# Two key pages per vector instruction in a decoder step

## The reference

```
h += W_o( sig(g_a) * U_a(stick-breaking attention) + sig(g_b) * U_b(GLA) )
h += PEER(rmsnorm(h))            # product-key experts: top 16 of 16384 for each of 8 heads
h += (p W_ple) * sigmoid(rmsnorm(h) W_ple_gate)
```

```
z[h, s]    = q[h] . k[s, h] / sqrt(64) + bias[h]
A[h, s]    = sigmoid(z[h, s]) * prod over later j of (1 - sigmoid(z[h, j]))
out[h]     = sum over s of A[h, s] * v[s, h]
```

## Time and profile before

| | us |
|---|---|
| median of 3 runs | 2529.41 (2528.65 to 2534.58) |
| the profiled execution | 2528.97 |
| its span, first to last instruction | 2527.3 |
| PE busy | 2043.2 |
| DVE busy | 1417.8 |
| POOL busy | 977.5 |
| ACT busy | 641.2 |

### The profile page before, as it was taken

One profiled execution on the slowest core, in us unless ns is written; L12 is line 12 of the kernel. 1 busy time (PEld: TensorE's weight loads), 2 busy tenths in 40 slices (PEclk: granted clock), 3 DMA queues, 4 the chain that ended last, 5 costly groups with the idle time before them and its releaser, 6 DMA issues.

```text
span 2527.3 us, 25588 instructions
## 1 busy us (share of the span) xinstructions
PE 2043.2 (81%) x6090; PEld 1018.0 (40%) x6090; DVE 1417.8 (56%) x2800; ACT 641.2 (25%) x1753; POOL 977.5 (39%) x1422
## 2 busy tenths in 40 slices
PE   7999965787778999947777777887778877688778
PEld 6746850143334738823232322333233333233322
DVE  3698898513211215976665556555566555666442
ACT  2202220201443012112233232232322332323321
POOL 0233333002222000025666555654555644566540
PEclk9999988977888999979999999999999999999999
DMA  3568779763443323149999999999999999999991
GB/s 120 182 206 287 253 259 350 252 194 118 140 153 132 103 68 113 50 167 413 408 418 421 422 388 413 386 385 420 421 387 411 368 422 422 385 404 400 372 422 58
DMA packets 139984, 738.89 MB, mean 292 GB/s; under 512 B 19112, under 2 KB 19544, under 8 KB 72312
## 3 DMA queue, kind: packets, MB, share of 16 engines
q0 software_dynamic: 105632, 645.98, 64.5%
q1 hardware_dynamic: 34272, 91.91, 10.9%
HBM read 732.26 MB, written 5.56 MB: 292 GB/s over the span
## 4 chain that ended last, share of the span: by engine, by line
PE 35%; DMA 25%; issue 13%; DVE 10%; POOL 6%; ACT 5%; POOLq 4%; SPq 1%; ACTq 0%; DVEq 0%
DMA arena<-experts_in,arena 22%; PE bank L1533 11%; DVE arena L121 6%; PE bank L1477 4%; POOLq L482 4%; POOL arena L507 4%; PE bank L1502 3%; PE bank L1440 3%; DVE arena L1148 3%; PE bank L1427 2%; ACT arena L121 2%; PE bank L1198 2%; POOL arena L503 1%; PE bank L1287 1%; DMA arena<-cache_v_in 1%
## 5 line engine op out<-in xcount | busy, mean ns | idle before, releaser
L1533 PE MATMUL bank<-arena 128*128 128x512 f32 x2048 | 980.7, 628 | 303.2 <-ACT arena L768 303.0
L1148 DVE CUSTOM_DVE_ANT_0 arena<-arena 128x1024 f32<-128x1024 f32 x512 | 626.5, 1230 | 537.7 <-DMA arena<-experts_in,arena 535.9
L1533 PEld LDWEIGHTS bank<-arena 128*128 128x128 f32 x2048 | 391.0, 198 | 889.9 <-ACT arena L768 465.5
L507 POOL DMA_INDIRECT arena<-experts_in,arena x512 | 593.3, 1159 | 130.9 <-issue 114.4
L503 POOL TENSOR_TENSOR arena<-arena 128x2 uint32<-128x2 uint32 x256 | 85.8, 335 | 728.4 <-PE bank L1533 413.1
L760 ACT ACTIVATE arena<-arena 128x2 f32<-128x2 f32 x256 | 52.1, 203 | 888.4 <-DVE arena L1148 888.4
L480 POOL DMA_DIRECT2D arena<-cache_k_in x256 | 137.4, 537 | 310.9 <-DVE arena L821 173.9
L1198 PE MATMUL bank<-arena 128*128 128x260 f32 x1024 | 228.1, 384 | 5.7 <-DVE arena L121 5.0
L1198 PEld LDWEIGHTS bank<-arena 128*128 128x128 f32 x1024 | 194.1, 190 | 40.0 <-issue 7.6
L835 DVE TENSOR_TENSOR arena<-arena 128x512 f32<-128x512 f32 x256 | 175.5, 686 | 50.7 <-DMA arena<-cache_k_in 48.1
L121 ACT ACTIVATE arena<-bank 128x260 f32<-128x260 f32 (+6 forms) x165 | 70.7, 447 | 448.9 <-PE bank L1477 102.8
(11 more groups left out here) (101 smaller groups left out, 1637.5 us busy)
## 6 DMA issues: line engine op xcount, KB each, us to landing
arena<-cache_k_in POOLq DMA_DIRECT2D x256, 256.0 KB, 4.8
arena<-w_stream_in SPq DMA_DIRECT2D x72, 512.0 KB, 3.7
arena<-cache_v_in SPq DMA_DIRECT2D x128, 256.0 KB, 4.2
arena<-cache_v_in POOLq DMA_DIRECT2D x128, 256.0 KB, 4.1
arena<-experts_in,arena POOLq DMA_INDIRECT x520, 9.9
arena<-w_ple_gate_in SPq DMA_DIRECT2D x1, 4096.0 KB, 12.9
arena<-xT_in SPq DMA_DIRECT2D x2, 1040.0 KB, 6.1
arena<-x_rows_in SPq DMA_DIRECT2D x1, 2048.0 KB
```

Of the source, the lines that this page charges most:

```text
L507: pool.indirect_dma_start(gring[:, s, :], None, A["experts"], bass.IndirectOffsetOnAxis(ap=slot_idx[:, s:s + 1], axis=0)).then_inc(g_lande ...
L1148: last = V.tensor_tensor_reduce(gring[:, s, 0:D], gring[:, s, 0:D], xn2[:, t], 1.0, 0.0, ALU.mult, ALU.add, dot[:, s:s + 1])
L1533: last = mm(bank[yb[c2]][:, :], diag[:, s], gring[:, s, D + 512 * c2:D + 512 * c2 + 512], start=False, stop=True, skip_group_check=True)
```

## The change

DVE now takes two pages per instruction. The multiply reads two slots of `kring` (1024 columns) and the query broadcast over both; the sum reads two buffers of `prod` and writes 2 x 8 numbers. `PRODS` counts pairs and is 2, so `prod` keeps its size. A multiply waits for both pages to have landed, and `k_free` rises by 2 with each sum. The wait for the multiply (`k_mul`) stands before the sum instead of before the next multiply. Since `zs` is in reversed order and a sum writes its two columns in rising order, POOL loads the later page of a pair into the even slot (`s ^ 1`).

```diff
-PRODS = 4
+PRODS = 2
...
-            ("xn", 8 * T), ("xT", 8 * T), ("kring", RING_K * PAGE_ROW), ("prod", PRODS * PAGE_ROW)])
+            ("xn", 8 * T), ("xT", 8 * T), ("kring", RING_K * PAGE_ROW), ("prod", 2 * PRODS * PAGE_ROW)])
...
-        prod = view("prod").rearrange("p (s c) -> p s c", s=PRODS)
+        prod = view("prod").rearrange("p (s c) -> p s c", s=2 * PRODS)
...
             with pool.Fori(0, NB * PAGES // RING_K) as i:
-                pages = [page_number(i * RING_K + s) for s in range(RING_K)]
+                pages = [page_number(i * RING_K + (s ^ 1)) for s in range(RING_K)]
                 for s in range(RING_K):
                     pool.wait_ge(k_free, i * RING_K + (s + 1))
                     load_page(kring, A["cache_k"], k_landed, pages[s], s)
...
-            def sum_heads(b, g, s):
-                V.tensor_reduce(z4[:, bass.ds(b, 1), bass.ds(g, 1), :].rearrange("p a c h -> p (a c h)"),
-                                prod[:, s % PRODS].rearrange("p (h d) -> p h d", h=H), AX.X, ALU.add).then_inc(k_free, 1)
+            def pair(ring, i):
+                return ring[:, 2 * i:2 * i + 2].rearrange("p u c -> p (u c)")
+
+            def sum_heads(b, g, i):
+                V.tensor_reduce(z4[:, bass.ds(b, 1), bass.ds(g, 2), :].rearrange("p a c h -> p (a c) h"),
+                                pair(prod, i % PRODS).rearrange("p (u h d) -> p u h d", u=2, d=HD), AX.X, ALU.add).then_inc(k_free, 2)
 
             def k_pages(samples, rounds):
 
                 begin = samples[0] == 0 and rounds[0] == 0
+                pairs = RING_K // 2
                 with dve.Fori(*samples) as b:
                     with dve.Fori(*rounds) as g:
-                        for s in range(RING_K):
-                            n = b * PAGES + g * RING_K
-                            dve.wait_ge(k_landed[s], b * (16 * PAGES // RING_K) + g * 16 + 16)
-                            dve.wait_ge(k_free, n + (RING_K if begin and s == 0 else RING_K + s + 1 - PRODS))
-                            if s:
-                                dve.wait_ge(k_mul, n + s)
-                            V.tensor_tensor(prod[:, s % PRODS], kring[:, s], qbc[:, bass.ds(b, 1), :].rearrange("p a n -> p (a n)"),
-                                            ALU.mult).then_inc(k_mul, 1)
-                            if s:
-                                sum_heads(b, g * -RING_K + (PAGES - s), s - 1)
-                        dve.wait_ge(k_mul, b * PAGES + g * RING_K + RING_K)
-                        sum_heads(b, g * -RING_K + (PAGES - RING_K), RING_K - 1)
+                        for i in range(pairs):
+                            for s in (2 * i, 2 * i + 1):
+                                dve.wait_ge(k_landed[s], b * (16 * PAGES // RING_K) + g * 16 + 16)
+                            dve.wait_ge(k_free, b * PAGES + g * RING_K + (RING_K if begin and i == 0 else RING_K + 2 * i + 2 - 2 * PRODS))
+                            q = qbc[:, bass.ds(b, 1), :].to_broadcast([P, 2, PAGE_ROW])
+                            V.tensor_tensor(prod[:, 2 * (i % PRODS):2 * (i % PRODS) + 2], kring[:, 2 * i:2 * i + 2], q, ALU.mult).then_inc(k_mul, 1)
+                            if i:
+                                dve.wait_ge(k_mul, b * (PAGES // 2) + g * pairs + i)
+                                sum_heads(b, g * -RING_K + (PAGES - 2 * i), i - 1)
+                        dve.wait_ge(k_mul, b * (PAGES // 2) + g * pairs + pairs)
+                        sum_heads(b, g * -RING_K + (PAGES - RING_K), pairs - 1)
```

## The result

The changed kernel takes 2544.72 us (median of 4 runs, 2542.75 to 2552.2) against 2529.03 for the one before in the same comparison: a ratio of 1.0064, interval 1.0038 to 1.009, 15.7 us slower. The profiled execution is the longest of the four, 2552.2 us, so its rows hold 23.2 us to explain against the profiled 2528.97, more than the medians do.

The account below looks back on a forecast made before the run. GpSimd was taken to pace the key rounds at 10.78 us each. Late ring slots 11.2 plus late landings 6.8 made 18 us: 2528.97 + 18 + 0.44 = 2547 us, range 2531 to 2562.

Parts of the forecast that it names:

- GpSimd paces, DVE is second: Key rounds (8 pages each): GpSimd's own floor is 10.78 us a round, DVE needs 9.70, second by 1.1 us.
- The faster rival: Key rounds: DVE is the true pace, so its 0.34 us a round saves 9.5 us: 2520 us; 9 in 100.
- The instructions: DVE on keys: pair instructions start 1.14 us apart, a stall costs 0.13, broadcast operand zero; 0.34 us a round saved.
- The ring: Key-page slots: slot 4 comes free only with slot 5, so GpSimd waits for x over 3.83; 11.2 us later.
- x: Key ring: time from a load's issue to the start of the multiply it releases; taken as 4.4 to 5.7 us.
- Landings unchanged: Key-page loads: median landings of the kernel before, 4.5, 5.7, 4.4 and 5.7 us in four stretches, used as x.
- the first rival: Key-page loads: landings get shorter because GpSimd's bursts are broken up, x about 4.0: 2533 us; 17 in 100.
- the term of 11.2: Key rounds: loss from late slots at median landings, 3.0 + 2.4 + 2.3 + 3.5 us over four stretches.
- 6.8 for late landings inside a burst: Key rounds: late landings that medians hide cost between none and 13.6 us; the middle, 6.8, was taken.
- The round after the head norms, not counted: First key round after the head norms: DVE paces GpSimd there anyway, so no loss was counted.
- PE takes the shift one for one: PE at `later_keys(2)`, after round 27: a later DVE moves PE and the end by the whole shift, 18 us.
- Rounds 28 to 31 hidden: Last key rounds: up to 3.8 us more, hidden because PE uses DVE's last scan 9.3 us after it ends.

Follow-up runs that it names:

- E7: Changed kernel with slots released when the pair's multiply ends and page numbers read without bounds checks: 2501.77 us, ratio 0.9898 to the kernel before.
- E1: Kernel before, single pages, but even page's multiply waits for both landings and k_free rises by 2 after the odd page's sum: 2544.14 us, ratio 1.0062.
- E4: Changed kernel with key-ring slots released when the pair's multiply ends instead of its sum: 2527.84 us, ratio 1.0009 to the kernel before.
- E3: Kernel before, single pages, with only the even page's multiply waiting for both landings: 2537.71 us, ratio 1.0041.
- E6: Changed kernel with page numbers read without bounds checks, slots still freed by the pair's sum: 2530.42 us, ratio 1.001 to the kernel before.

## Why the prediction held

The time (2547 against 2544.7) and the path were right. That the two numbers agree within 3 us is in part luck: two terms were off by several us in opposite directions, and one that was left out was not nothing.
- **GpSimd paces, DVE is second.** Right for the kernel before. DVE fell to 9.32 us a round and the time rose; DVE's pace shows in E7, after GpSimd's floor was lowered and slots were released early. The faster rival had DVE as the pace and fell here. In the changed kernel neither of the two floors is the pace but the ring between them (12.04 us a round).
- **The instructions.** 1.13 to 1.14 us and stalls of 0.12 (1.25 - 1.13), against 1.14 and 0.13: right, and the broadcast operand costs nothing visible. The Trainium skill, VectorE: DVE Perf Modes, section on the TRN2 errata, says that a large tile pays the fixed latency once and many small ones pay it each time. The trace agrees: 1.14 us for two pages at once against 2 x 0.60 us. The rule says nothing of who waits for DVE, and the forecast by it alone would have had the wrong sign.
- **The ring.** Slot 4 is where GpSimd stands most, as computed, and a late slot shifts the page numbers behind it. The second gap was expected before slot 6; it is before slot 2, where the formula has no wait for an x under 4.9, and makes 7.2 us of rounds 6 to 26 beside slot 4's 12.4. E1 shows the two couplings alone to be sufficient, E4 that early release removes the loss.
- **Landings unchanged.** Wrong. The medians in the changed kernel, for 83:200, 200:250, 250:350 and 350:442 us, against the earlier trace rows:

```profile
arena<-cache_k_in POOLq DMA_DIRECT2D x72, 256.0 KB, 4.1
...
arena<-cache_k_in POOLq DMA_DIRECT2D x32, 256.0 KB, 4.6
...
arena<-cache_k_in POOLq DMA_DIRECT2D x64, 256.0 KB, 4.0
...
arena<-cache_k_in POOLq DMA_DIRECT2D x64, 256.0 KB, 4.5
```

  All four are shorter, 5.7 became 4.6 and 4.5, as the first rival said, and they are so in E1 too (3.9, 4.6, 4.2 and 5.0). That the spreading of the loads is the reason was not tried by itself. With these medians as x my own formula gives 1.2 + 1.5 + 0.7 + 2.0 = 5.4 us, less the 3.5 that the kernel before lost: 2 us in place of 11.2. But a median landing is not the x of the formula, which runs to the start of the multiply. Read from the first load and first multiply of each round, x in rounds 6 to 26 is 4.53 us on average before; in the changed kernel it is 5.13 with the 0.665 for the second page, 4.47 without. Put in round by round, it gives 8.2 us, less 2.1 that the kernel before loses: 6.1 of the 17.4 us that these rounds lost. So the term of 11.2 was too large, and the rest, 6.8 for late landings inside a burst, too small. E3 fits that: waiting for both pages alone costs 10.8 us. How the 15.7 us of the medians divide between the two is open.
- **The round after the head norms, not counted.** Wrong, by 3.9 us of the profiled execution: from 127.17 to 150.06 it was 22.9 us, from 130.59 to 157.43 it is 26.8. The round behind it gives 1.0 us back (12.9 against 13.9).

```profile
130.59 1.20 POOL L480 DMA_DIRECT2D arena<-cache_k_in  x2 [5.55 <-issue]
...
157.43 1.21 POOL L480 DMA_DIRECT2D arena<-cache_k_in  x2 [20.02 <-DVE arena L824]
```

  When DVE comes back, the first slot is released by a sum that ends 3.50 us after the first multiply starts instead of 2.0, and DVE had come to the norms later too.
- **PE takes the shift one for one.** Right within the scatter: 24.4 us at the wait and 23.2 in the execution, 17.2 and 16.5 in E1. In E3 and E6, though, 7.3 and 7.4 us at the wait are only 1.9 and 2.3 in the execution. What lies behind `later_keys(2)` takes 2103.8 to 2110.9 us in the ten executions, whatever the keys did, so a single execution says this only to a few us.
- **Rounds 28 to 31 hidden.** Right: PE reaches `later_keys(3)` without idle time, at 503.18, DVE's last scan having ended at 494.27 + 1.22.

```profile
494.27 1.22 DVE L121 TENSOR_TENSOR_SCAN arena<-arena 128x512 f32<-128x512 f32 x1
```

```profile
503.18 1.12 PE L1259 MATMUL bank<-arena 128*128 128x512 f32 x2
```

## What to carry to other kernels

A ring has a round-trip time as well as a rate: issue, landing, use and release of one slot must fit into the time in which the loader comes round to it, and grouping two slots per instruction adds one slot to the start and one instruction to the end of that trip. So work out that slack per slot before making instructions larger, release a slot at its last reader rather than at the end of the work on it, and look for the pace where the gaps are constant (here 5.52 us of register reads on the loading queue) even if the profile names another engine beside them. Here two small edits, to when the queue may load and to how it reads page numbers, were worth 1.0%, and the wide instructions neither helped nor hurt once they were in.

## What the runs showed of the hardware

GpSimd's queue pauses once before the 114th and once before the 220th load of this stage, for about 2.6 us beyond the normal distance of two loads, in all ten traces and wherever it stands in time. In the kernel before and in E7:

```profile
254.59 0.54 POOL L480 DMA_DIRECT2D arena<-cache_k_in  x1 [5.52 <-issue]
257.90 2.54 POOL L480 DMA_DIRECT2D arena<-cache_k_in  x4 [2.78 <-DVE arena L821]
```

```profile
242.00 0.54 POOL L480 DMA_DIRECT2D arena<-cache_k_in  x1 [3.56 <-DVE arena L839]
245.32 4.52 POOL L480 DMA_DIRECT2D arena<-cache_k_in  x7 [2.78 <-issue]
```

The name beside the first gap of 2.78 us is a sum of DVE that had ended long before. The 128 value loads that follow in the same queue have one such pause as well, before their own 114th, in all ten traces. In the kernel before:

```profile
779.48 0.54 POOL L480 DMA_DIRECT2D arena<-cache_v_in  x1 [5.54 <-issue]
782.72 4.52 POOL L480 DMA_DIRECT2D arena<-cache_v_in  x7 [2.71 <-issue]
```

The cause was not tried; that it follows the count of loads and not the time or the kernel is all that is shown.

A read of a page number into a register takes about 0.63 us from one to the next with its bounds (the table read 0.288, its register operations 0.152 and 0.046, the assertion 0.018, the rest between them) and about 0.40 without. From the gaps it is (5.52 - 3.56)/8 = 0.245 us less for each. In these traces no load is issued while the eight reads run.
